# Decoder layer with hierarchical MoE: the two expert rows of a token are gathered by index in three waves during the last blocks, instead of tile by tile after the last scatter

## The reference, cut to what matters

```python
h = rmsnorm(x, g_ffn)
# hier_moe: one group of 4, in it the best 2 of 8 experts, weights w2
g = argmax(h @ router_group_w + b)                # group
e1, e2 = top2((h @ router_expert_w + b)[g])       # two of 32 experts
out = w2[0] * expert(e1, h) + w2[1] * expert(e2, h)
# expert(e, h) = (silu(h @ gate[e]) * (h @ up[e])) @ down[e]   (1024 -> 128 -> 1024)
x = x + out
y = rmsnorm(x, g_final)
```

## Time and profile before

| | |
|---|---|
| median of 3 runs | 609.39 us (609.37 to 610.42) |
| the profiled execution's own time | 608.55 us |
| its span in the profile | 606.5 us |
| PE busy | 571.4 us, 94% of the span |
| DVE busy | 439.9 us, 73% |
| ACT busy | 242.2 us, 40% |
| POOL busy | 88.5 us, 15% |
| mean granted clock of PE | 0.981 of full |
| moved | 111.27 MB, mean 183 GB/s |

### The profile page before, as it was taken

How to read it: one execution, slowest core, us unless ns; L and a number is a source line. 1 busy time by engine, 2 the same in 40 slices (tenths; PEclk the granted TensorE clock), 3 DMA queues, 4 the chain that set the end, 5 groups by cost and what they waited for, 6 DMA issues and landing times.

```text
span 606.5 us, 9765 instructions
## 1 busy us (share of the span) xinstructions
PE 571.4 (94%) x3401; PEld 473.4 (78%) x3401; DVE 439.9 (73%) x749; ACT 242.2 (40%) x389; POOL 88.5 (15%) x136
## 2 busy tenths in 40 slices
PE   8899999999999999899999995899997999999775
PEld 6799999997899889688888874777654768887222
DVE  4937997999999696746666658899731667786285
ACT  6642112222212427322222116576322567775443
POOL 4300000200000000100000000433331334431000
PEclk9999999999999999999999997899998999999889
DMA  8761210131112202455422107699989999962697
GB/s 317 150 123 38 69 36 1 36 93 35 36 36 79 105 36 69 114 203 198 157 80 93 54 36 247 215 332 404 392 329 412 407 352 395 394 241 97 209 421 299
DMA packets 52598, 111.27 MB, mean 183 GB/s; under 512 B 10867, under 2 KB 29176, under 8 KB 51449
## 3 DMA queue, kind: packets, MB, share of 16 engines
q1 hardware_dynamic: 44773, 92.18, 43.2%
q0 software_dynamic: 7168, 17.84, 8.2%
q10 hardware_dynamic: 596, 0.50, 0.3%
HBM read 96.36 MB, written 21.86 MB: 195 GB/s over the span
## 4 chain that ended last, share of the span: by engine, by line
PE 51%; DVE 17%; DMA 7%; issue 3%; ACT 2%; SPq 1%; POOL 0%; POOLq 0%; DVEq 0%; ACTq 0%
PE ps L2259 14%; PE ps L2081 9%; PE ps L2425 6%; PE ps L2364 3%; PE ps L2386 3%; PE ps L2400 3%; PE ps L2401 3%; PE ps L2402 3%; DMA at_opair_p<-scratch_out 3%; DMA at_wlater<-in_expert_w_down 3%; DVE at_mixP L1360 3%; PE ps L2496 2%; PE ps L2323 2%; DVE at_hT L1319 1%; DVE at_lnsq L1546 1%
## 5 line engine op out<-in xcount | busy, mean ns | idle before, releaser
L2081 PE MATMUL ps<-at_hT,at_ring 128*128 128x384 f32 x936 | 165.5, 333 | 0.0
L2081 PEld LDWEIGHTS ps<-at_hT,at_ring 128*128 128x128 f32 x936 | 155.9, 188 | 5.1 <-issue 5.0
L2259 PE MATMUL ps<-at_hT,at_mring 128*128 128x512 f32 (+1 forms) x432 | 102.7, 393 | 2.0 <-DVE at_mring L1514 1.3
L2259 PEld LDWEIGHTS ps<-at_hT,at_mring 128*128 128x128 f32 (+1 forms) x432 | 77.3, 182 | 21.3 <-DVE at_mring L1514 1.7
L1360 DVE SCALAR_TENSOR_TENSOR at_mixP<-at_uc,at_par,at_mixP 128x1024 f32<-128x1024 f32 x60 | 77.1, 1285 | 2.1
L2400 PE MATMUL ps<-at_whi,at_hTm 128*128 128x256 f32 x176 | 51.0, 290 | 0.0
L2402 PE MATMUL ps<-at_whi,at_hTm_lo 128*128 128x256 f32 x176 | 49.1, 279 | 0.0
L2364 PEld LDWEIGHTS ps<-sb_ident,at_xg 128*128 128x128 f32 x232 | 29.3, 192 | 18.2 <-issue 15.2
L1795 DVE TENSOR_TENSOR at_wlater_lo<-at_wlater,at_whi 128x1024 fp32r<-128x1024 f32 x30 | 36.7, 1225 | 6.0 <-ACT at_whi L988 5.1
L2425 PE MATMUL ps<-at_wlater,at_actT 128*128 128x512 f32 (+1 forms) x92 | 38.0, 597 | 0.7 <-ACT at_actT L1003 0.7
L988 ACT ACTIVATE at_whi<-at_wlater 128x1024 fp32r<-128x1024 f32 x30 | 31.6, 1055 | 7.3 <-PE ps L2402 6.5
(11 more groups left out here) (324 smaller groups left out, 919.2 us busy)
## 6 DMA issues: line engine op xcount, KB each, us to landing
at_wlater<-in_expert_w_gate SPq DMA_DIRECT2D x20, 512.0 KB, 11.1
at_wlater<-in_expert_w_up SPq DMA_DIRECT2D x20, 512.0 KB, 12.8
at_wlater<-in_expert_w_down SPq DMA_DIRECT2D x20, 512.0 KB, 15.4
at_raw<-in_w_in SPq DMA_DIRECT2D x16, 512.0 KB, 4.0
at_opair_p<-scratch_out SPq DMA_DIRECT2D x8, 1024.0 KB, 14.7
at_wfirst<-in_expert_w_gate SPq DMA_DIRECT2D x12, 512.0 KB, 9.0
at_wfirst<-in_expert_w_up SPq DMA_DIRECT2D x12, 512.0 KB, 10.0
at_wfirst<-in_expert_w_down SPq DMA_DIRECT2D x12, 512.0 KB, 12.5
```

The costliest lines, as they stand in the source:

```text
L2081: mm = pe.matmul(ps[:, bank + r, 0:t1 - t0], w[:, wpart, k * P:(k + 1) * P], hT[:, hpart, k, t0:t1], start=(m, wpart, hpart) == (0, 0, 0), ...
L2259: mm = pe.matmul(ps[0:n, b + r, :], mring[:, 1 - i % 2, mpart, k * P:k * P + n], wo[:, wpart, k, r * 512:(r + 1) * 512], start=(c, mpart, ...
```

## The change

Two index lists are made on DVE. `soon` has the tokens whose two experts both belong to a block that is scattered by the time of the token's wave, `later` has the others; in each list the rest are out of bounds. If there are overflow blocks, no token is in `soon`. POOL gathers pairs (8 KB rows of `scratch_out`) by `soon` in three waves: tiles 8, 0, 1 when blocks up to 23 are scattered; 2, 3, 4 when up to 24; 7 and 5 when up to 25. Each wave is issued behind the scatter of the block that follows. After `moe_done` POOL gathers the rest by `later`, for eight tiles. Tile 6 is loaded whole by SP, once tile 1 is complete.

The pair buffers move to slots of weights that are no longer needed. `scratch_out` is filled with input rows at the start (ten transfers on SP, between the pieces), so that no gather reads unwritten memory. The last four scatters always have 128 rows. The overflow counts are computed on all 128 partitions instead of one, with the same instructions.

```diff
+EARLY = [[8, 0, 1], [2, 3, 4], [7, 5]]
+WAVES = len(EARLY)
+WHOLE = [6]
...
+def wave_after(n):
+    return NB - 3 - WAVES + n
...
-        opair_p = at("opair_p", [P, SB, 2 * D], o_hT)
-        opair_s = at("opair_s", [P, 2 * D], o_x1)
+        opair_a = at("opair_a", [P, 4, 2 * D], o_x1)
+        opair_b = at("opair_b", [P, TILES - 4, 2 * D], o_hT)
...
+            def fill_out(n):
+                r = n * 256 % NP
+                for src, at_, count in ((a["x_prompt"][0, r:r + 256, :], n * 256, 256),) if n < 8 else tuple(
+                        (a["x_sample"].rearrange("b t d -> (b t) d"), 2 * NP + h * NS, NS) for h in range(2)):
+                    sp.dma_start(orow[at_:at_ + count, :], src).then_inc(s["out_filled"], 16)
             for p in range(2, NPIECE):
                 load_piece(p)
+                if 5 <= p < 14:
+                    fill_out(p - 5)
...
-            sp.wait_ge(s["moe_done"], 1)
-            for i in FINAL:
-                n = rows(i)
-                src = orow[2 * i * P:2 * (i * P + n), :].rearrange("(t k) d -> t (k d)", k=2)
-                sp.dma_start(opair(i)[0:n, :], src).then_inc(pair_in[i], 16)
+            sp.wait_ge(pair_in[FINAL[2]], 32)
+            for i in WHOLE:
+                src = orow[2 * i * P:2 * (i + 1) * P, :].rearrange("(t k) d -> t (k d)", k=2)
+                sp.dma_start(opair(i), src).then_inc(pair_in[i], 16)
...
-                if is_pair(b):
+                if is_pair(b) or NB - 4 <= b < NB:
                     move(P)
...
+            def pair_rows(i, index):
+                g.indirect_dma_start(opair(i), None, pairs,
+                                     bass.IndirectOffsetOnAxis(ap=index[:, i:i + 1], axis=0),
+                                     bounds_check=last_token, oob_is_err=False).then_inc(pair_in[i], 16)
+            def early_pairs(n):
+                pool.wait_ge(s["turns_ready"], 1)
+                for k in range(2):
+                    pool.wait_ge(scat[k], 16 * ((wave_after(n) + 2 - k) // 2))
+                for i in EARLY[n]:
+                    pair_rows(i, soon)
...
                 if b >= 1:
                     scatter(b - 1, columns(b - 1)[1])
+                if 0 <= b - 2 - wave_after(0) < WAVES:
+                    early_pairs(b - 2 - wave_after(0))
...
             over_from(0)
+            pool.wait_ge(s["moe_done"], 1)
+            for i in FINAL:
+                if i not in WHOLE:
+                    pair_rows(i, later)
...
+            def pair_turns():
+                do(v.memset(turn[:, 0:FIX], 0.0))
+                do(v.tensor_copy(turn[:, FIX:NE], pos))
+                shape = [P, TILES * 2, NE]
+                w = both[:].rearrange("p t k e -> p (t k) e")
+                chosen = eidx[:].rearrange("p t k -> p (t k)").unsqueeze(2).broadcast_to(shape)
+                do(tt(w, io32[:].unsqueeze(1).broadcast_to(shape), chosen, ALU.is_equal))
+                do(tt(w, w, turn[:].unsqueeze(1).broadcast_to(shape), ALU.mult))
+            def pair_latest():
+                do(v.tensor_reduce(latest[:], both[:], AX_X, ALU.add))
+                do(tt(done_by[:], latest[:, :, 0], latest[:, :, 1], ALU.max))
+                do(ts(no_over[:], incl[:, NE - 1:NE], 0.5, None, ALU.is_le))
+                do(ts(token[:], pid[:, :, 0], 0.5, -0.5, ALU.mult, ALU.add))
+            def pair_lists():
+                for n in range(WAVES):
+                    last_turn = place(wave_after(n)) - FIX + 0.5
+                    for i in EARLY[n]:
+                        do(ts(done_by[:, i:i + 1], done_by[:, i:i + 1], last_turn, no_over[:], ALU.is_le,
+                              ALU.mult))
+                do(stt(later[:], done_by[:], float(NONE), token[:], ALU.mult, ALU.add))
+                do(ts(done_by[:], done_by[:], -float(NONE), float(NONE), ALU.mult, ALU.add))
+                do(tt(soon[:], done_by[:], token[:], ALU.add), s["turns_ready"])
-            between = {1: expert_order, ...
+            between = {11: pair_turns, 12: pair_latest, 13: pair_lists, 1: expert_order, ...
...
-                dve.wait_ge(pair_in[i], 16)
+                dve.wait_ge(pair_in[i], 16 if i in WHOLE else 32)
...
-                pe.wait_ge(pair_in[i], 16)
+                pe.wait_ge(pair_in[i], 16 if i in WHOLE else 32)
```

More of the change, by code:

```diff
@@ L294, in build_layer @@
         order = at("order", [P, 8, REST], o_state + 2304)
+        both = at("both", [P, TILES, 2, NE], o_state)
+        turn = at("turn", [P, NE], o_state + 2304)
+        latest = at("latest", [P, TILES, 2], o_state + 2304 + 192)
+        done_by = at("done_by", [P, TILES], o_state + 2304 + 288)
+        token = at("token", [P, TILES], o_state + 2304 + 384)
+        soon = at("soon", [P, TILES], o_state + 2304 + 480, I32)
+        later = at("later", [P, TILES], o_state + 2304 + 672, I32)
+        no_over = at("no_over", [P, 1], o_state + 2304 + 736)
         eid = at("eid", [1, REST], o_state + 3072, I32)
@@ L596, in expert_block @@
                     sp.wait_ge(s["d_done"], i * LAP + max(done_in(NE + j - LAP), NB + j - LAP) + 1)
+                    for t in EARLY[min(j // 2, WAVES - 1)]:
+                        sp.wait_ge(pair_in[t], 16)
                 load_expert(i, j, e, first)
@@ L1709, in _ @@
             do(v.memset(flat[:], 0.0))
+            do(v.memset(eidx[:], 0.0))
             for i in range(LAST):
@@ L1865, in overflow_counts @@
             def overflow_counts():
-                do(ts(ovi[:], carry[0:1, :], float(P - 1), None, ALU.add))
+                do(ts(ovi[:], carry[:], float(P - 1), None, ALU.add))
                 do(ts(ovi[:], ovi[:], 7, None, ALU.logical_shift_right))
@@ L1872, in overflow_counts @@
                 do(v.memset(again[:], 0.0))
-                do(ts(few[0:1, :], pos[0:1, :], LIGHT - 0.5, None, ALU.is_le))
-                do(stt(again[:, FIX:NE], rest[0:1, :], 64.0, few[0:1, :], ALU.is_gt, ALU.mult))
-                do(ts(few[0:1, :], pos[0:1, :], LIGHT + LARGE - 0.5, -1.0, ALU.is_ge, ALU.add))
-                do(stt(run[0:1, :], rest[0:1, :], P + 64.5, few[0:1, :], ALU.is_le, ALU.mult))
-                do(stt(few[0:1, :], pos[0:1, :], LIGHT - 0.5, run[0:1, :], ALU.is_ge, ALU.mult))
-                do(stt(n_e[:, FIX:NE], few[0:1, :], 1.0, n_e[:, FIX:NE], ALU.add, ALU.mult))
+                do(ts(few, pos, LIGHT - 0.5, None, ALU.is_le))
+                do(stt(again[:, FIX:NE], rest, 64.0, few, ALU.is_gt, ALU.mult))
+                do(ts(few, pos, LIGHT + LARGE - 0.5, -1.0, ALU.is_ge, ALU.add))
+                do(stt(run, rest, P + 64.5, few, ALU.is_le, ALU.mult))
+                do(stt(few, pos, LIGHT - 0.5, run, ALU.is_ge, ALU.mult))
+                do(stt(n_e[:, FIX:NE], few, 1.0, n_e[:, FIX:NE], ALU.add, ALU.mult))
                 do(tt(n_e, n_e, again[:, 0:NE], ALU.add))
-                do(v.tensor_tensor_scan(incl, ones[0:1, 0:NE], n_e, 0.0, ALU.mult, ALU.add))
+                do(v.tensor_tensor_scan(incl, ones[:, 0:NE], n_e, 0.0, ALU.mult, ALU.add))
                 do(tt(ovm[:], n_e, again[:, 1:NE + 1], ALU.add))
```

31 lines of the change are left out of this document (17 added, 14 removed).

## The result

The changed kernel takes 615.17 us (median of 4 runs, 613.42 to 615.35), the kernel before beside it 609.48 us (609.37 to 610.42): a ratio of 1.0088, 95% interval 1.0067 to 1.0108. Forecast were 605.3 us and a range of 603.0 to 609.2: wrong, in size and in sign. The profiled execution took 615.35 us, its span is 613.3 us.

What follows compares the result with a forecast made beforehand. 8.9 MB of expert rows loaded behind the last scatter bound the tail. With most loaded early, DVE starts at 573.6 and ends 25.7 later at 599.3; 604.5 us profiled, median 605.3, range 603.0 to 609.2.

Steps and rivals of the forecast that it cites:

- DVE's first addition: Start of DVE's tail, forecast at 567.3 + 0.8 + 1.5 + 4.0 = 573.6, against 572.59 before.
- (c): "All scattered" on POOL comes later because scatters share the queue with early rows: 0.8 us, bounds 0 and 7.5.
- Rival 3: Early gathers on POOL push out the last scatters, 8 KB rows perhaps costing two descriptors: up to 612.0 us; chance 0.10.
- g: POOL's time for each early gather, taken as 1.4 us; scatter 28 is late only from 1.67.
- (a): POOL jumps over the nested overflow blocks before the final gathers: 1.5 us, bounds 0 and 4.45.
- one jump, not three turns: Argument against POOL's jump costing all 4.45 us: DVE and PE pass three loop turns, POOL one jump.
- (b): Landing of the first final gather behind "all scattered": 4.0 us, bounds 3.3 and 8.0.
- The edits at nothing: Scratch fills on SP, DVE's lists, 128-row scatters and moved buffers cost nothing; fills 0 to 1 us, lists at worst 0.7.
- DVE's chain: From the start of tile 8's addition to the end of the last norm: 25.7 us, against 30.8 before.
- Behind it 3.1 us in the span: From DVE's last norm to the end of the span: 3.1 us, unchanged from before.
- the prediction's 6240 rows: Rows counted for the kernel before in 58 indirect transfers; with 928 completions, the 7168 packets of the software queue.

Runs made afterwards that it cites:

- e8: The changed kernel again, with no edit: 613.96 us, ratio 1.0070 to the kernel before.
- e2: The changed kernel with its eight early gathers issued but no token in them; all rows of eight tiles come by the final gathers: 619.24 us, ratio 1.0152.
- e10: The changed kernel with block 28's result in a buffer of its own, so its copies don't wait for scatter 26: 615.54 us, ratio 1.0088.
- e5: The changed kernel with POOL's early gathers replaced by SP loading six whole tiles on its own hardware queue, at the same three moments: 613.34 us, ratio 1.0053.
- e4: The changed kernel with one early wave, of tiles 4, 7, 5, behind scatter 24; SP loads the six others whole: 611.51 us, ratio 1.0008.
- e3: The changed kernel with a copy of the final gathers inside the branch taken without overflow blocks, so POOL doesn't jump first: 611.26 us, ratio 1.0009.
- e1: The changed kernel without any gather of pairs; SP loads all nine tiles after "all scattered"; fills, lists, moved buffers and 128-row scatters stay: 608.99 us, ratio 0.9980.
- e6: The changed kernel with one early wave, of tiles 8, 0, 1, 2; SP loads the other five once tile 8 is in: 612.81 us, ratio 1.0031.
- e7: e6 without POOL's jump ahead of the final gathers: 610.42 us, ratio 0.9994.
- e12: The changed kernel with one early wave, of tiles 8, 0, 1, no jump, and six direct loads by SP, tile 2 first: 607.59 us, ratio 0.9971.
- e9: e7 with SP's five direct loads issued only behind tile 2, in the order 4, 3, 7, 5, 6: 613.83 us, ratio 1.0068.
- e11: The changed kernel with two early waves (8, 0, 1 and 2, 3), no jump, four direct loads behind tile 2: 610.96 us, ratio 1.0022.

## Why the prediction was wrong

DVE's first addition was forecast at 573.6 and came at 584.28; the rest of the sum held. The 10.7 us are, in the prediction's own steps (0.2 more lie in small gaps):

- **(c), "all scattered", the step that failed.** Forecast 0.8 late, measured 5.4 (e8: 4.9): 4.6 us of the miss. I had seen the competition for the queue, and mis-sized it. The windows 550 to 574 moved 7.3 MB (9 x 265, 12 x 348 and 3 x 239 kB) where I reckoned 6.8. A full share moves 0.355 MB/us, not the 0.39 that I had divided out of a share of 0.27 in quiet windows; 7.3 MB take 20.5 us at it instead of 17.4. And the engines are not full from the start: 0.80 over the first nine us (0.72 from 547 to 564, where the prediction wanted 0.8 or more), since the waves wait for scatters which themselves now land late (8.1 us for scatter 25 in e8's chain, against 3.3 to 4.5 for the last five of before). I gave that 1.6 us in all. e2 shows that it is the bytes and not the issues, e10 that it is not the buffers, e5 that the larger part is not POOL's queue but what lies under it. How much is their volume and how much the place of the later waves is open (e4).
- **Rival 3 had the right end by the wrong mechanism.** It made POOL's issue of 8 KB rows the bound from g = 2.3; g is 1.35, below my own 1.4. With its bounds tied to g alone, the range for (c) was empty between 0.8 and the dear issue that the rows spoke against. A rival "the last scatters land as under full traffic", 7.2 us in the median and 9.3 at most by the times that stood in the earlier trace rows, would have given 7.2 - 4.0 to 9.3 - 4.0, 3.2 to 5.3 us in place of 0.8: from a gain of 1.7 us to none.
- **(a), the jump.** Taken 1.5, bounds 0 and 4.45; measured 3.27 before the first gather, against 0.27 in e3 without it: 1.8 us of the miss. Against my "one jump, not three turns", it was worth nearly the gap that PE showed (3.82).
- **(b), the landing.** 4.46 against 4.0: 0.5. Right within its bounds.
- **What had come ahead of scatter 24:** 3.6 us, which the prediction had as nothing. Scatter 24 varies by 5 us over profiles with the same front, so a part is chance. Taking the tails off the differences of the medians leaves 2.5 us in the first runs (615.17 - 609.48 - 3.2) and 0.6 in the later (613.96 - 610.40 - 3.0). How much of that the fills and lists cost is not shown; the fills took 6.0 us in the median, where 5 was reckoned. In the first profile the end of the projection agrees with before, and the loss falls at block 0 and at blocks 12 and 13, where the granted clock was 0.80 (384 to 388 us) and 0.76 (469 to 476 us) of full, and before 1.00 in both windows.
- **DVE's chain:** 25.9 us (584.28 to 610.18) against 25.7. Right, and no wait over 1.68 in it. Behind it 3.1 us in the span. Right.
- **The edits at nothing:** right within about 1 us, by e1.

So the gain was made (DVE's chain of 30.8 us became 25.9; beside e1's 28.4, with direct loads and the same front, it is 2.5) and more than spent: 5.4 us on late scatters and 3.3 + 4.5 us between "all scattered" and DVE, where before SP's direct load needed 5.3.

## What to carry to other kernels

A quiet stretch of DMA ahead of the critical transfer isn't free room: the small transfers on the critical path there land fast because it is quiet. Size the prefetch against the landing time of the last of them, with the rate at full load, and fill with the part that is wanted first; here one wave of 1.5 to 2.1 MB left "all scattered" on time (e4, e6, e7, e12) and 5.3 MB in three waves cost 5 us. Free it wasn't even then: scatter 25, behind the small wave, landed 6.8 to 7.0 us after its issue (e6, e7, e12) instead of 4.5, only nothing waited long for it. And ask what an engine passes on its way to a newly placed instruction: the way over unused code cost 3.0 us, where the landing of the gather took 4.5. Last, measure the bare rearrangement too: e1, which prefetches nothing, can't be told by its interval from the best version that does.

## What the hardware showed unexpectedly

**Code is fetched over the same DMA engines.** At the end of the blocks PE goes over its unused overflow code to its own rows. That gap "by issue" is 3.3 to 3.8 us wherever the engines are quiet by then (before, e1, e2, e4, e6, e7, e9, e11, e12) and 5.3 to 6.7 us wherever the early bytes are still moving, on either queue (the changed kernel, e8, e3, e5, e10). The changed kernel, and e4:

```profile
573.16 9.45 PE L2558 MATMUL ps<-at_x,sb_ident 128*128 128x512 f32 x16 [6.69 <-issue]
```

```profile
569.35 10.15 PE L2560 MATMUL ps<-at_x,sb_ident 128*128 128x512 f32 x16 [3.42 <-issue]
```

The queues of the stretch 556 to 575 of the changed kernel (packets, MB, share of 16 engines) have the code as transfers of their own, of 16 KiB each on q8 and 8 KiB on q14, beside 5.92 MB of rows:

```profile
q0 software_dynamic: 1434, 5.92, 87.1%
q8 instruction: 3, 0.05, 1.0%
q14 instruction: 3, 0.02, 0.3%
```

The Trainium skill (Runtime: NRT & Kernel Launch, Instruction fetch mechanics) says that each sequencer fetches its code through a DMA queue of its own in blocks of 16 KiB, and that this is mostly hidden in straight code. The trace has such transfers, of 16 KiB on q8; q14's are 8 KiB, and other queues with code it does not show. That PE's gap is longer because its code waits behind the rows fits all fourteen profiles, but no run isolates it.

**ACT stands still at block 26 in six profiles, and why is open.** It is idle 1.7 us before its silu in the changed kernel's first profile, e2 and e3, where e1 has 0.3, and 1.8 to 3.3 us at the same block in e9, e10 and e11; there is no such stall in before, e1, e4 to e8 and e12. The nearest thought is a fetch of ACT's own code behind full engines. The rows speak against it: e2 has the stall though its waves move no rows, and e8 has none though it is the same program as the changed kernel. In e9 the queues of the 3.3 us in which ACT stands still (556.6 to 559.9) show no transfer of code:

```profile
q0 software_dynamic: 258, 1.05, 93.1%
```

**Gathers of 8 KB rows take POOL no longer than those of 4 KB** (1.0 us and 0.3 ahead), and rows out of bounds cost nothing that e2 could tell beyond the issue. They are not without a trace, though. The 17.84 MB of the software queue before are 4352 rows of 4 KB; the other 1888 of the prediction's 6240 rows are indices out of bounds, and each leaves a packet of 4 bytes. And an 8 KB row is one packet, not two as rival 3 feared: the changed kernel has 960 packets of 8192 bytes for its 960 pair rows.
